# Modulation rows of a transformer-and-expert kernel computed as columns and carried to all partitions through DRAM

## The chip, the cores and the metric

The kernel runs on one core of a Trainium2 chip. The metric is the device time of one execution in microseconds (us); less is better. The kernel before takes 2819.86 us (median of 3 runs, 2818.37 to 2821.85).

## The reference

Two blocks follow each other on 256 tokens of width 1024 in float32. The first block has two layers of three sublayers (feed-forward, mixer, feed-forward) with keys and values shared from a stage between the layers. The second has a convolution, a differential attention and, after each of the two, a layer of experts chosen by keys (16384 experts, 16 per head, 8 heads). Each sublayer is modulated: from a conditioning vector c a shift, a scale and a gate of 1024 values each are computed by a product with a wide matrix.

```python
mods = jnp.split(c_act @ cond_w[layer] + cond_b[layer], 3 * N_SUBLAYERS, axis=-1)

def sublayer(x, shift, scale, gate, g_pre, g_post, fn, res_weight):
    h = rmsnorm(x, g_pre) * (1 + scale[:, None, :]) + shift[:, None, :]
    return x + res_weight * gate[:, None, :] * rmsnorm(fn(h), g_post)

def ada_mod(c, w, b):                                   # second block
    m = jax.nn.silu(c) @ w + b
    shift, scale, gate = jnp.split(m, 3, axis=-1)
    return shift[:, None, :], 1.0 + scale[:, None, :], 1.0 + gate[:, None, :]
    ...
    h = x * scale + shift
    x = layer_norm(DEEPNORM_ALPHA * x + gate * f, ln_g[i, 0], ln_b[i, 0])
```

The change concerns how these shifts, scales and gates are computed and brought to where they are used. Nothing else of the arithmetic changes.

## The kernel before, in words

**Stages.** The program is a list of stages numbered 0 to 7: feed-forward (0), gated linear attention (1), feed-forward (2), the shared keys and values (3), feed-forward (4), latent attention (5), feed-forward (6), convolution (7). A tail holds the experts (8), the attention (9) and the experts again (10). A feed-forward stage streams 11 tiles of 2 MB of gate-and-up weights and then 6 tiles of down weights through a ring of four slots in SBUF. SyncE issues these loads (`fill`, L561). TensorE computes 22 "units" of 16 matmuls each into three PSUM banks `psW` in turn (the loop with L955), and then the product with the down weights (`project`, L894). ScalarE applies the activation (L1599) and VectorE multiplies gate and up (L2194) and so frees the bank (`unit_stored`).

**Modulation work.** The product of c with the wide matrix is cut into 60 pieces of 512 outputs (1024 x 512 weights, 2 MB), and each piece into two halves of 1 MB. The table `beside` says beside which feed-forward stage (0, 2, 4 or 6) a piece is computed: 16, 14, 14 and 16 pieces. GpSimd issues the loads of the halves into three 1 MB buffers (`modulation_weights`, L496 and L500; two in `mring`, one in `M`), each after the half that was there three halves ago has been used (`m_used`). VectorE computes them between its multiplications, four halves in three units (`halves_done`, `half_step`). A piece is named (stage, j): j = 0, 1 is the shift, 2, 3 the scale, 4, 5 the gate.

There are two ways to compute a piece:

- **As a column** (32 pieces: shift and scale of stages 1 to 7 and 9). The weights come transposed, outputs on the partitions. `half_column` runs two operations of 128 x 1024 with an accumulated sum (L2048), which give two columns of 128 outputs each, and adds the bias columns (L2052). The result lies in `col`, eight values per partition for a vector of 1024, and is used where features lie on the partitions.
- **As a row** (28 pieces: all gates, and all of stages 8 and 10). VectorE accumulates eight products of 128 x 512 in `macc` (L2028, L2030) and adds the bias in one partition (L2035). What remains is a sum over the 128 partitions, which TensorE makes with a matmul against a matrix of ones, so that the sum lands in all partitions of the bank `psM`. For the 18 pieces used in stages 0 to 8 this is `sum_row` (L744), placed between units of the feed-forward stage or inside `project`, and VectorE moves the result to its place in `M` (`store_row`, L2097 and L2100, for a gate of stages 0 to 6 with the norm gain that GpSimd spread there before, `gate_gain`, L549). For the last 10 pieces ("late") the matmuls (L1396) stand in the first phase of the tail and ScalarE moves the result (`late_row`).

**Tail.** GpSimd issues 512 gathers of 1 MB (L662) into eight buffers, each after the one before in its buffer has been used; VectorE makes dot products (L2536), ScalarE weights them (L1722 to L1729), TensorE sums the gathered rows (L1303). Other work of TensorE (queries, attention) is interleaved.

The order on each engine is the order of the program text. The waits between engines are semaphores.

Of the kernel before, what the change touches and what calls it, by code (L numbers as in the profile page):

```python
# [29 lines left out]
F32 = mybir.dt.float32  # L30
# [55 lines left out]

class Turn:
# [33 lines left out]
def _program(nc, ctx, a, out, stages):  # L121
# [20 lines left out]
    small = sb("small", [P, 320])  # L142
# [80 lines left out]
    given_cols = arena[:, 14080:14296]  # L223
    cond_row = [M[:, 0, 0, :], p_diag[:].rearrange("p n t -> p (n t)")]
    col_bias = given_cols[:, 0:160].rearrange("p (n v k) -> p n v k", n=10, v=2)
    col_gain = given_cols[:, 160:216].rearrange("p (n k) -> p n k", n=7)
    col = small[:, 160:320].rearrange("p (n v k) -> p n v k", n=10, v=2)
# [29 lines left out]
    b_loaded = [sem(f"b_loaded{i}") for i in range(2)]  # L257
    g_loaded = [sem(f"g_loaded{i}") for i in range(2)]
    ln_loaded = sem("ln_loaded")
# [7 lines left out]
    m_stored = sem("m_stored")  # L267
# [36 lines left out]
    late_summed = sem("late_summed")  # L304
    late_stored = sem("late_stored")
# [139 lines left out]
    def mod_bias(st):  # L445
        n = st.n
        if n < 7:
            layer, s = (0, n) if n < 3 else (1, n - 4)
            return a["cond_b"][layer][3 * D * s:3 * D * (s + 1)]
        i, m = divmod(n - 7, 2)  # L450
        return a["ada_b_2"][i, m]


    def rows_of(n, lo, hi):
        return [(every[n], j) for j in range(lo, hi)]

    beside = {0: rows_of(0, 4, 6) + rows_of(1, 0, 6) + rows_of(2, 0, 4) + rows_of(3, 0, 4),
              2: rows_of(2, 4, 6) + rows_of(4, 0, 4) + rows_of(5, 4, 6) + rows_of(5, 0, 4) + rows_of(8, 2, 4),
              4: rows_of(4, 4, 6) + rows_of(6, 0, 4) + rows_of(7, 0, 4) + rows_of(9, 0, 4),
              6: rows_of(6, 4, 6) + rows_of(7, 4, 6) + rows_of(8, 4, 6) + rows_of(9, 4, 6) + rows_of(8, 0, 2)  # L460
              + rows_of(10, 0, 6)}
    pieces = [row for n in (0, 2, 4, 6) for row in beside[n]]
    as_row = [j >= 4 or st.n in (8, 10) for st, j in pieces]
    row_pieces = [piece for piece, row in zip(pieces, as_row) if row]
    col_pieces = [piece for piece, row in zip(pieces, as_row) if not row]
    late_pieces = [(st, j) for st, j in row_pieces if st.n > 8 or (st.n == 8 and j >= 4)]
    summed_pieces = [piece for piece in row_pieces if piece not in late_pieces]

    def rows_before(st):
        return sum(piece in summed_pieces for n, rows in beside.items() if n < st.n for piece in rows)  # L470

    def row_count(st, j):
        return summed_pieces.index((st, j)) + 1

    def col_count(st):

        return 4 + 2 * (col_pieces.index((st, 3)) + 1) if st.n else 4


    def halves_done(st, unit):  # L480

        return min(2 * len(beside[st.n]), max(unit - 1, 0) * 4 // 3)

    def row_at(st, unit):

        return sum(piece in summed_pieces and 2 * r + 2 <= halves_done(st, unit - 2) for r, piece in enumerate(beside[st.n]))
# [4 lines left out]
    def modulation_weights(eng, i):  # L491

        st, j = pieces[i // 2 - 1] if i >= 2 else (stages[0], 0)
        q = i % 2
        if i >= 2 and (st, j) in col_pieces:
            eng.dma_start(half_rows[i % HALVES].rearrange("p k n -> p (k n)"), a["mod_t"][2 * col_pieces.index((st, j)) + q])\  # L496
                .then_inc(m_loaded[i % HALVES], 16)
            return
        r = 4 + row_pieces.index((st, j)) if i >= 2 else 0
        eng.dma_start(half_rows[i % HALVES].rearrange("p k n -> p (k n)"), a["row_t"][r, :, 2048 * q:2048 * (q + 1)])\  # L500
            .then_inc(m_loaded[i % HALVES], 16)
# [11 lines left out]
    def bias_row(eng, n):  # L513
        st, j = pieces[n]
        r = sum(as_row[:n])
        b = mod_bias(st).rearrange("(o n) -> o n", o=1)
        if r >= 2:
            before = [i for i in range(n) if as_row[i]][r - 2]
            eng.wait_ge(m_used, 2 * before + 4)
        eng.dma_start(brow[0:1, r % 2, :], b[:, HALF * j:HALF * (j + 1)])\  # L520
            .then_inc(b_loaded[r % 2], 16)

    def row_target(st, j):

        kind = j // 2
        if st.n >= 9:
            m = (M_at, M_p1)[st.n - 9][:, kind]
        elif st.n == 8 and kind == 2:
            m = M_at[:, 0]
        else:  # L530
            m = M[:, st.n % 2, kind]
        return m[:, (j % 2) * HALF:(j % 2 + 1) * HALF]
# [7 lines left out]
    gate_before = {2: 0, 4: 2, 5: 1, 6: 4}  # L540
    gates_loaded = {0: 16, 2: 32, 4: 48, 6: 64, 1: 16, 5: 32}

    def gate_gain(eng, st):

        par = st.n % 2
        if st.n in gate_before:
            eng.wait_ge(x_ready, x_count(gate_before[st.n] + 1))
# [121 lines left out]
    def _(pool):  # L669
# [28 lines left out]
        for n, (st, j) in enumerate(pieces):  # L698
            if st.n < 7 and j == 4:
                gate_gain(pool, st)  # L700
# [3 lines left out]
            if as_row[n]:  # L704
                bias_row(pool, n)
# [2094 lines left out]
```

## Time and profile before

| | us |
|---|---|
| Runs: median (lowest, highest) | 2819.86 (2818.37, 2821.85) |
| Profiled execution, span from first to last instruction | 2816.4 |
| TensorE matmul busy | 2553.4 (91%) |
| VectorE busy | 1565.9 (56%) |
| ScalarE busy | 635.3 |
| GpSimd busy | 668.6 |
| DMA, mean over the span | 333 GB/s, 938.33 MB |

The span is the only time that the profile gives for its execution; the runs' median is 3.5 us above it. A busy share says how long an engine works, not whether the program waits for it; that is read from the chain that ended last. Stages 0 to 7 fill the time up to about 1376 us; the tail fills the rest.

### The profile page before, as it was taken

How to read it: one execution, taken by the hardware profiler on the slowest of the kernel's cores; microseconds unless marked ns; L12 is line 12 of the kernel's file. 1: busy time of each engine (PE TensorE's matmuls, PEld its weight loads, DVE VectorE, ACT ScalarE, POOL GpSimd, SP SyncE). 2: the span in 40 equal slices, each digit the busy share in tenths (PEclk: the TensorE clock that was granted, in tenths of full speed). 3: DMA queues.
4: the chain of work that ended last, by engine and by line, in shares of the span. 5: the costliest groups of instructions: out<-in, count | busy, mean ns of one | idle time of the engine just before them, and what ended most of it. 6: DMA issues, size and time to landing. Idle time of an engine off the chain costs nothing.

```text
span 2816.4 us, 26912 instructions
## 1 busy us (share of the span) xinstructions
PE 2553.4 (91%) x9987; PEld 1595.6 (57%) x9987; DVE 1565.9 (56%) x3441; ACT 635.3 (23%) x1837; POOL 668.6 (24%) x687
## 2 busy tenths in 40 slices
PE   8999999999999999999999887999869989777776
PEld 6874558856884678758665333645425636322222
DVE  4562135524451546713688875365785666974544
ACT  1001210001000220000133433253333533332222
POOL 1110000100010001100243444243443333544332
PEclk9999999999999999999999999999999999999999
DMA  9894426845783548946799999999999999999997
GB/s 394 346 363 146 190 93 262 354 183 202 298 350 132 194 157 338 358 174 260 299 392 421 421 422 421 406 418 421 421 422 402 421 421 414 422 401 421 421 422 326
DMA packets 120409, 938.33 MB, mean 333 GB/s; under 512 B 14765, under 2 KB 16197, under 8 KB 18902
## 3 DMA queue, kind: packets, MB, share of 16 engines
q0 software_dynamic: 93344, 669.09, 58.5%
q1 hardware_dynamic: 26934, 267.52, 24.1%
q8 instruction: 79, 1.29, 0.2%
q14 instruction: 52, 0.43, 0.0%
HBM read 935.50 MB, written 1.05 MB: 333 GB/s over the span
## 4 chain that ended last, share of the span: by engine, by line
PE 65%; DMA 21%; DVE 7%; ACT 3%; issue 2%; SPq 1%; POOL 1%; DVEq 0%
PE psW L955 20%; DMA ring<-in_peer_uv_dram,lamt 19%; PE psF L1303 14%; PE psF L894 11%; PE psW L1414 4%; DVE ring L2536 3%; PE psW L864 2%; PE psW L834 2%; PE psW L1322 2%; PE psW L823 2%; PE psF L930 1%; PE psW L875 1%; PE psW L1426 1%; DMA mring<-in_tail_w_dram 1%; PE psF L1173 1%
## 5 line engine op out<-in xcount | busy, mean ns | idle before, releaser
L1303 PE MATMUL psF<-ring,p_diag 128*128 128x512 f32 x2048 | 954.2, 611 | 210.1 <-ACT p_diag L1729 208.1
L2536 DVE SCALAR_TENSOR_TENSOR ring<-ring,h 128x1024 f32<-128x1024 f32 x512 | 621.3, 1224 | 426.7 <-DMA ring<-in_peer_uv_dram,lamt 423.2
L662 POOL DMA_INDIRECT ring<-in_peer_uv_dram,lamt x512 | 579.7, 1132 | 1018.6 <-PE psF L1303 800.9
L1303 PEld LDWEIGHTS psF<-ring,p_diag 128*128 128x128 f32 x2048 | 378.8, 193 | 730.1 <-issue 392.4
L955 PE MATMUL psW<-hT,ring 128*128 128x256 f32 x2560 | 555.9, 379 | 0.1
L955 PEld LDWEIGHTS psW<-hT,ring 128*128 128x128 f32 x2560 | 486.1, 190 | 73.0 <-issue 7.7
L894 PE MATMUL psF<-ring,arena 128*128 128x512 f32 x704 | 303.5, 593 | 4.1 <-DVE arena L2194 4.1
L894 PEld LDWEIGHTS psF<-ring,arena 128*128 128x128 f32 x704 | 133.4, 190 | 172.1 <-issue 166.5
L1722 ACT ACTIVATE small<-small 128x2 f32<-128x2 f32 x255 | 51.6, 202 | 649.9 <-DVE ring L2536 649.8
L1729 ACT ACTIVATE p_diag<-ident,small 128x128 f32<-128x128 f32 x510 | 176.9, 394 | 8.3
L1599 ACT ACTIVATE arena<-psW 128x256 f32<-128x256 f32 x88 | 33.8, 384 | 595.8 <-PE psW L955 535.9
L2194 DVE TENSOR_TENSOR arena<-arena,psW 128x256 f32<-128x256 f32 x80 | 33.7, 421 | 234.4 <-ACT arena L1599 234.0
L1414 PEld LDWEIGHTS psW<-hT,mring 128*128 128x128 f32 x1024 | 120.3, 194 | 19.6 <-issue 11.5
L1414 PE MATMUL psW<-hT,mring 128*128 128x128 f32 x1024 | 121.3, 277 | 5.3 <-DMA mring<-in_tail_w_dram 5.2
L1725 ACT ACTIVATE small<-small,gout 128x1 f32<-128x1 f32 x510 | 122.4, 287 | 8.3
L500 POOL DMA_DIRECT2D mring<-in_row_t_dram x39 | 22.3, 572 | 342.8 <-DVE macc L2030 301.2
L2148 DVE RECIPROCAL small<-small 128x1 f32<-128x1 f32 x12 | 1.9, 155 | 182.0 <-ACT small L1584 182.0
L2048 DVE SCALAR_TENSOR_TENSOR mring<-mring,M 128x1024 f32<-128x1024 f32 x66 | 78.1, 1220 | 2.6 <-DMA mring<-in_mod_t_dram 2.6
L2000 DVE COPY arena<-psW 128x512 f32<-128x512 f32 (+5 forms) x48 | 29.9, 628 | 88.3 <-PE psW L864 52.3
L834 PE MATMUL psW<-hT,ring 128*128 128x128 f32 x640 | 73.8, 276 | 5.2 <-DVE hT L2112 5.2
L1583 ACT ACTIVATE h<-psF 128x1024 f32<-128x1024 f32 x12 | 12.3, 1025 | 293.5 <-PE psF L894 256.7
L834 PEld LDWEIGHTS psW<-hT,ring 128*128 128x128 f32 x640 | 72.2, 192 | 7.0 <-issue 4.0
(329 smaller groups left out, 2249.0 us busy)
## 6 DMA issues: line engine op xcount, KB each, us to landing
ring<-in_gu_t_dram SPq DMA_DIRECT2D x44, 2048.0 KB, 9.0
mring<-in_tail_w_dram SPq DMA_DIRECT2D x50, 1024.0 KB, 9.1
mring<-in_mod_t_dram POOLq DMA_DIRECT2D x43, 1024.0 KB, 7.0
ring<-in_down_t_dram SPq DMA_DIRECT2D x20, 2048.0 KB, 8.6
mring<-in_row_t_dram POOLq DMA_DIRECT2D x39, 1024.0 KB, 7.5
ring<-in_conv_in_t_dram SPq DMA_DIRECT2D x12, 2048.0 KB, 7.5
M<-in_mod_t_dram POOLq DMA_DIRECT2D x21, 1024.0 KB, 6.8
M<-in_row_t_dram POOLq DMA_DIRECT2D x19, 1024.0 KB, 7.5
```

The lines of the kernel that those rows point to most:

```text
L662: pool.indirect_dma_start(out=pair(n % PAIRS), out_offset=None, in_=rows, in_offset=bass.IndirectOffsetOnAxis(ap=s_idx[:, c:c + 1], axis=0 ...
L823: ins = pe.matmul(ps[:, t * P:(t + 1) * P], w[:, k, t * P:(t + 1) * P], hT[:, k, b * P:(b + 1) * P], start=(k == 0), stop=(k == KD - 1))
L834: ins = pe.matmul(ps[:, t * P:(t + 1) * P], w[:, k, t * P:(t + 1) * P], hT[:, k, b * P:(b + 1) * P], start=(k == t == 0), stop=(k == KD - ...
L864: ins = pe.matmul(ps[:, 0:n], lhs[:, k, b * P:(b + 1) * P], w[:, k, 0:n], start=(k == 0), stop=(k == kd - 1))
L894: ins = pe.matmul(psF[:, b, f * HALF:(f + 1) * HALF], lhs[:, k, b * P:(b + 1) * P], w[:, k % 4, f * HALF:(f + 1) * HALF], start=(k == 0), ...
L955: ins = pe.matmul(ps[:, part * T:(part + 1) * T], w[:, k, part * 256 + c * P:part * 256 + (c + 1) * P], hT[:, k, :], start=(k == 0), stop= ...
L1303: ins = pe.matmul(psF[:, b, f * HALF:(f + 1) * HALF], p_diag[:, n % PAIRS, :], row_v(n % PAIRS)[:, f * HALF:(f + 1) * HALF], start=(i == 0 ...
L1414: ins = pe.matmul(ps[:, t * P:(t + 1) * P], w[:, k, t * P:(t + 1) * P], hT[:, k, b * P:(b + 1) * P], start=(k == 0), stop=(k == KD - 1))
L1725: act.activation(p_w[:, c + s:c + s + 1], p_gel[:, c + s:c + s + 1], ACT.Copy, scale=s_g[:, b, i + s:i + s + 1]).then_inc(w_ready, 1)
L1729: act.activation(p_diag[:, c + s, :], ident[:], ACT.Copy, scale=p_w[:, c + s:c + s + 1])\
L2048: ins = dve.scalar_tensor_tensor(w[:, t, :], w[:, t, :], 1.0, cond_row[st.n >= 7], ALU.mult, ALU.mult, accum_out=dst[:, t:t + 1])
L2536: dve.scalar_tensor_tensor(row_u(c), row_u(c), 1.0, h[:, b, :], ALU.mult, ALU.mult, accum_out=p_dots[:, c:c + 1]).then_inc(dot_done, 1)
```

## The change

The 28 row pieces become column pieces: all 60 are computed by `half_column`. The bias columns and the norm gains of the gates (`col_post`) come with the other given columns, now 376 values per partition and not 216, and in `brow`. A vector that is needed in all partitions (14 of them, the table `ROWS`) is then written by GpSimd from `col` to a row of 4 KB in DRAM (`write_row`; eight values per partition that lie 512 bytes apart in DRAM, so 1024 separate elements) and read back to 128 partitions (`spread_row`, 512 KB). The matmuls with ones, `store_row`, `late_row`, the 28 bias loads and the 6 loads of `gate_gain` go away.

```diff
-    gate_before = {2: 0, 4: 2, 5: 1, 6: 4}
+    gate_before = {2: 0, 4: 2, 5: 1, 6: 4, 7: 5}
+ROWS = ((0, 2), (1, 2), (2, 2), (5, 2), (4, 2), (6, 2), (7, 2), (8, 2), (9, 2), (8, 0), (8, 1), (10, 0), (10, 1), (10, 2))
...
-    given_cols = arena[:, 14080:14296]
+    given_cols = brow[:].rearrange("p v n -> p (v n)")[:, 0:376]
...
+    def write_row(eng, r):
+
+        n, kind = ROWS[r]
+        eng.wait_ge(col_stored, 4 + 2 * (row_done(r) + 1))
+        eng.dma_start(a["rows"][r, :].rearrange("(k p) -> p k", p=P), col[:, n, kind, :],
+                      allow_slow_non_contiguous=True).then_inc(row_written, 16)
+
+    def spread_row(eng, r):
+
+        n, kind = ROWS[r]
+        eng.wait_ge(row_written, 16 * (r + 1))
+        if kind == 2 and n in gate_before:
+            eng.wait_ge(x_ready, x_count(gate_before[n] + 1))
+        eng.dma_start(row_target(n, kind), a["rows"][r:r + 1, :].to_broadcast([P, D])).then_inc(row_landed(n, kind), 16)
...
-        for n, (st, j) in enumerate(pieces):
-            if st.n < 7 and j == 4:
-                gate_gain(pool, st)
...
-            if as_row[n]:
-                bias_row(pool, n)
...
+        for n, piece in enumerate(PIECES + [None] * 4):
...
+            if piece:
+                for i in (2 * n + 2, 2 * n + 3):
+                    if i >= HALVES:
+                        pool.wait_ge(m_used, i - HALVES + 1)
+                    modulation_weights(pool, i)
+            if spread < written:
+                spread_row(pool, spread)
+                spread += 1
+            if written < len(ROWS) and row_done(written) <= n - 2:
+                write_row(pool, written)
+                written += 1
...
-        def sum_row():
-
-            n = rows_taken.n
-            row_bank()
-            pe.wait_ge(m_used, 2 * pieces.index(summed_pieces[n]) + 4)
-            pe.matmul(psM[:], ones[:], macc[:, n % 2, :], start=True, stop=True).then_inc(m_reduced, 1)
-            rows_taken.next()
...
-                    sums_at(st, 2 * s + c)
...
-                pe.matmul(psM[:], ones[:], row_target(st, j), start=True, stop=True).then_inc(late_summed, 1)
...
+            half_column(halves_taken.n + 2, every[PIECES[n][0]], PIECES[n][1], q)
...
+            if kind == 2 and st.n < 7:
+                link(ins)
+                ins = dve.scalar_tensor_tensor(dst, dst, 0.5 if st.kind == "ffn" else 1.0, col_post[:, st.n, k:k + 2],
+                                               ALU.mult, ALU.mult)
...
-            dve.wait_ge(m_stored, row_count(st, 5))
+            dve.wait_ge(g_loaded[par], gates_loaded[st.n])
```

**TensorE, in the feed-forward stage 0.** `psW0` to `psW2` are the banks of the units; `macc` holds a piece's products, `psM` their sum. Before:

```order
L955 MATMUL psW2<-hT,ring 128x256 x16
L955 MATMUL psW0<-hT,ring 128x256 x16
L744 MATMUL psM<-macc,ones 128x512
L955 MATMUL psW1<-hT,ring 128x256 x16
L744 MATMUL psM<-macc,ones 128x512
L955 MATMUL psW2<-hT,ring 128x256 x16
```

And in the changed kernel (L916 is the line that was L955):

```order
L916 MATMUL psW2<-hT,ring 128x256 x16
L916 MATMUL psW0<-hT,ring 128x256 x16
L916 MATMUL psW1<-hT,ring 128x256 x16
L916 MATMUL psW2<-hT,ring 128x256 x16
L916 MATMUL psW0<-hT,ring 128x256 x16
```

The two sums between units are gone, and nothing stands in their place. The same holds at all 18 places.

**GpSimd, in stage 6, where most vectors are carried.** In brackets stands the semaphore that the instruction waits for. Before, the loads of weights alternate with the 2 KB loads of biases:

```order
L520 DMA brow<-in_ada_b_2_dram 1x16x32 [waits m_used]
L500 DMA M<-in_row_t_dram 128x2048 [waits m_used]
L500 DMA mring<-in_row_t_dram 128x2048 [waits m_used]
L520 DMA brow<-in_ada_b_2_dram 1x16x32 [waits m_used]
L500 DMA mring<-in_row_t_dram 128x2048 [waits m_used]
L500 DMA M<-in_row_t_dram 128x2048 [waits m_used]
```

In the changed kernel the writes to DRAM (L523) and the reads to all partitions (L532) stand between them:

```order
L523 DMA modulation_rows<-small 128x8x1 [waits col_stored]
L477 DMA mring<-in_mod_t_dram 128x2048 [waits m_used] x2
L532 DMA M<-modulation_rows 128x1024 [waits row_written]
L523 DMA modulation_rows<-small 128x8x1 [waits col_stored]
L477 DMA M<-in_mod_t_dram 128x2048 [waits m_used]
L477 DMA mring<-in_mod_t_dram 128x2048 [waits m_used]
L532 DMA M<-modulation_rows 128x1024 [waits row_written]
L523 DMA modulation_rows<-small 128x8x1 [waits col_stored]
```

A read waits on GpSimd's queue until its write has landed, and the next loads of weights stand behind it.

## Rows read from the trace of the kernel before

**Rows 1.** The page: busy time, share of the span, instructions of each engine.
```profile
PE 2553.4 (91%) x9987; PEld 1595.6 (57%) x9987; DVE 1565.9 (56%) x3441; ACT 635.3 (23%) x1837; POOL 668.6 (24%) x687
```

**Rows 2.** The chain that ended last, stage 0: start us, us, what.
```profile
31.63 19.58 DMA ring<-in_gu_t_dram
...
51.25 27.89 PE psW L955 x128
79.14 0.86 PE psM L744 x2
80.00 6.91 PE psW L955 x32
86.91 0.86 PE psM L744 x2
```

**Rows 3.** The same chain in stage 6, at its last two sums.
```profile
1145.88 0.86 PE psM L744 x2
1146.74 6.91 PE psW L955 x32
1153.65 0.86 PE psM L744 x2
```

**Rows 4.** Costliest groups: the sums on TensorE, of stages 0 to 6 and late.
```profile
L744 PE MATMUL psM<-macc,ones 128*128 128x512 f32 x36 | 18.4, 592 | 0.0
...
L1396 PE MATMUL psM<-arena,ones 128*128 128x512 f32 x20 | 10.2, 592 | 0.0
```

**Rows 5.** Stretches of the tail: length, busy us of each engine, clock, DMA share, GB/s.
```profile
1600.00:1650.00 50.00, 40.76 (x91) 16.11 (x90) 45.79 (x147) 18.95 (x57) 25.12 (x21) 1.00 1.01 421
...
1700.00:1750.00 50.00, 35.92 (x78) 13.80 (x77) 30.36 (x48) 16.62 (x53) 21.24 (x20) 1.00 1.01 421
```

**Rows 6.** Groups by shape: column operations and row operations on VectorE.
```profile
L2048 DVE SCALAR_TENSOR_TENSOR mring<-mring,M 128x1024 f32<-128x1024 f32 x66 | 78.1, 1220 | 2.6 <-DMA mring<-in_mod_t_dram 2.6
...
L2030 DVE SCALAR_TENSOR_TENSOR macc<-mring,cact,macc 128x512 f32<-128x512 f32 x82 | 61.6, 751 | 2.8
...
L2052 DVE TENSOR_TENSOR small<-small,arena 128x2 f32<-128x2 f32 x64 | 10.3, 160 | 2.2
...
L2035 DVE TENSOR_TENSOR macc<-macc,brow 1x512 f32<-1x512 f32 x18 | 12.2, 680 | 0.6
...
L2028 DVE TENSOR_SCALAR macc<-mring,cact 128x512 f32<-128x512 f32 x14 | 6.7, 480 | 0.0
...
L2100 DVE SCALAR_TENSOR_TENSOR M<-psM,M 128x512 f32<-128x512 f32 x12 | 8.3, 691 | 0.1
```

**Rows 7.** VectorE in order of time, one unit of stage 4 with two column halves.
```profile
813.77 0.42 DVE L2194 TENSOR_TENSOR arena<-arena,psW 128x256 f32<-128x256 f32 x1 [4.00 <-ACT arena L1599]
814.11 1.22 DVE L2048 SCALAR_TENSOR_TENSOR M<-M,p_diag 128x1024 f32<-128x1024 f32 x1
...
819.01 0.16 DVE L2052 TENSOR_TENSOR small<-small,arena 128x2 f32<-128x2 f32 x1
820.67 0.42 DVE L2194 TENSOR_TENSOR arena<-arena,psW 128x256 f32<-128x256 f32 x1 [1.51 <-ACT arena L1599]
...
827.92 1.22 DVE L2048 SCALAR_TENSOR_TENSOR M<-M,p_diag 128x1024 f32<-128x1024 f32 x1
```

**Rows 8.** GpSimd in order of time: a load of weights and its wait.
```profile
816.77 0.53 POOL L496 DMA_DIRECT2D M<-in_mod_t_dram  x1 [6.38 <-DVE M L2048]
```

**Rows 9.** Issue to landing of L496's loads, L549's and L520's, one line each.
```profile
DMA to landing us min/median/max: 5.0/7.0/10.5
...
DMA to landing us min/median/max: 4.7/6.9/9.0
...
DMA to landing us min/median/max: 1.7/5.7/20.0
```

**Rows 10.** DMA from 1 to 4 us, small packets: queue: packets, MB, share.
```profile
q1 hardware_dynamic: 298, 0.02, 6.6%
```

**Rows 11.** The page: GpSimd's queue: packets, MB, share of 16 engines.
```profile
q0 software_dynamic: 93344, 669.09, 58.5%
```

**Rows 12.** GpSimd: a bias load of 16 pieces and the first gather.
```profile
31.64 0.52 POOL L520 DMA_DIRECT2D brow<-in_cond_b_dram  x1
...
1361.31 1.02 POOL L662 DMA_INDIRECT ring<-in_peer_uv_dram,lamt  x1 [170.41 <-DVE lamt L2516]
```

**Rows 13.** Stage 6 while the pieces run, as in rows 5.
```profile
1050.00:1200.00 150.00, 148.97 (x625) 118.23 (x624) 103.35 (x155) 6.91 (x18) 22.98 (x42) 1.00 0.90 350
```

**Rows 14.** TensorE in order of time, last work before the first row of rows 2 lands.
```profile
43.80 7.38 PE L834 MATMUL psW<-hT,ring 128*128 128x128 f32 x64 [0.54 <-DVE hT L2112]
```

More of the change, by code:

```diff
@@ L442, in output_done @@
             eng.wait_ge(w_used, outputs[st.w + LOADS[st.kind] - 1])
[L445 to L473, printed above, removed]
     def col_count(st):
-        return 4 + 2 * (col_pieces.index((st, 3)) + 1) if st.n else 4
+        return 4 + 2 * (PIECES.index((st.n, 3)) + 1) if st.n else 4
     def halves_done(st, unit):
-        return min(2 * len(beside[st.n]), max(unit - 1, 0) * 4 // 3)
-    def row_at(st, unit):
-        return sum(piece in summed_pieces and 2 * r + 2 <= halves_done(st, unit - 2) for r, piece in enumerate(beside[st.n]))
+        return min(2 * len(BESIDE[st.n]), max(unit - 1, 0) * 4 // 3)
     def have_weights(eng, i):
@@ L491, in modulation_weights @@
     def modulation_weights(eng, i):
[L493 to L501, printed above, removed]
+        if i >= 2:
+            w = a["mod_t"][i - 2]
+        else:
+            w = a["row_t"][0, :, 2048 * i:2048 * (i + 1)]
+        eng.dma_start(half_rows[i % HALVES].rearrange("p k n -> p (k n)"), w).then_inc(m_loaded[i % HALVES], 16)
     def first_row(n):
@@ L511, in first_weights, with row_done, row_target, row_landed @@
                 .then_inc(first_loaded[n + q if n == 3 else n], 16)
[L513 to L532, printed above, removed]
+    def row_done(r):
+        n, kind = ROWS[r]
+        return PIECES.index((n, 2 * kind + 1))
+    def row_target(n, kind):
+        if n >= 9:
+            return (M_at, M_p1)[n - 9][:, kind]
+        if n == 8:
+            return M_at[:, 0] if kind == 2 else M[:, 0, kind]
+        return M[:, n % 2, 2]
+    def row_landed(n, kind):
+        if n >= 9 or (n == 8 and kind == 2):
+            return late_rows_loaded
+        return next_rows_loaded if n == 8 else g_loaded[n % 2]
+    late_rows = sum(n >= 9 or (n == 8 and kind == 2) for n, kind in ROWS)
     def norm_rows(eng, n, landed):
@@ L757, in sum_columns @@
             ins.then_inc(m_reduced, 1)
-        def sums_at(st, unit):
-            for _ in range(row_at(st, unit) - row_at(st, unit - 1)):
-                sum_row()
         def first_modulation(n):
@@ L904, in project @@
                     ins.then_inc(w_used, 1)
-                if k % 4 == 3:
-                    late = rows_taken.n - rows_before(st)
-                    if k == 3:
-                        late = row_at(st, FT + 1) - late
-                    else:
-                        late = min(1, sum(piece in summed_pieces for piece in beside[st.n]) - late)
-                    for _ in range(late):
-                        sum_row()
             for b in range(TB):
```

161 lines of the change are left out of this document (41 added, 120 removed).

## The prediction

> **What bounds the kernel now.** I read the page first, then the chain that ended last, then the groups by shape, and at the end GpSimd's queue and the DMA in the stretches where the change puts work. TensorE is busy 91% of the span [rows 1], but that is a mean over two halves with different limits. In stages 0 to 7, up to about 1376 us, the chain is almost all TensorE: units of 6.91 us follow each other without a gap, and the sums over partitions are links of that chain, 0.86 us each [rows 2, 3]. In the tail the same look shows another bound: whether TensorE is busy 40.76 of 50 us, with late sums, or 35.92, without them, the DMA share is 1.01 and the rate 421 GB/s [rows 5]. There the gathers set the pace.
>
> **The sums that go, on TensorE.** The group of the sums has 36 records, two for each matmul, so 18 matmuls [rows 4]. All 18 stand in the chain, from 79.14 us in stage 0 to 1153.65 us in stage 6 [rows 2, 3]: 4 in stage 0, 6 in stage 2, 2 in stage 4, 6 in stage 6. Each puts the next unit 0.86 us later (80.00 less 79.14). When one goes, what is late next is again a unit of TensorE: VectorE sat idle for 4.00 us before the multiplication of a unit, and with two halves in the unit before still for 1.51 us [rows 7], so it follows a TensorE that is 0.86 us earlier. 18 x 0.86 = 15.5 us. I take all of it.
>
> **The late sums.** 20 records are 10 matmuls [rows 4], at 0.86 us each 8.6 us, and as many moves on ScalarE. They lie where DMA runs at 421 GB/s before, during and after them [rows 5]. The bytes of the tail do not change, so I take 0; the other end is 8.6 us of gain, if the stretch were bound by TensorE's order in spots.
>
> **VectorE.** A row piece costs one operation of 0.48, seven of 0.751 and a bias of 0.68, together 6.4 us; a column piece costs four of 1.220, four accumulator reads of 0.08 and two bias adds of 0.16, together 5.5 us [rows 6]. Over 28 pieces that is 179.6 less 154.8 us (the sum of the removed groups by their counts, 196 x 0.751 + 28 x 0.48 + 28 x 0.68, and 28 x 5.53). The 18 moves out of `psM` at 0.69 go too, 12.4 us [rows 6], and 24 small multiplications by the norm gain at 0.16 come, 3.8 us. Busy time falls by about 33 us, to about 1532. It is worth nothing by itself: VectorE waits for ScalarE and that for TensorE in each unit [rows 7].
>
> **GpSimd's queue and the DMA.** 28 bias issues of 0.5 us and 6 loads of 512 KB go; 14 writes and 14 reads of 512 KB come. The read is of the shape of the removed gain load: 0.53 us to issue, landed after 6.9 us [rows 9]. In stages 0, 2 and 4 there are as many reads as there were gain loads (2, 2, 1); in stage 6 there are 9 for 1. So stage 6 alone gets 8 x 0.524 = 4.2 MB more. It moves 350 GB/s at a share of 0.90 over 150 us [rows 13]; 28 GB/s more gives 0.97. That fits, with little room.
>
> The write is the operation that the trace does not show: 1024 elements of 4 bytes. From below: small packets cost 0.066 x 16 x 3 us / 298 = 10.6 ns each [rows 10], so 64 per engine take 0.7 us, and a 2 KB bias load landed after 5.7 us at the median, 1.7 at least [rows 9]. From above: the mean packet of GpSimd's queue costs 0.585 x 16 x 2816.4 / 93344 = 282 ns [rows 11]; at that price one write holds all engines for 18 us. I take the small packets, which are the nearer row in size: 1 us of the engines, landed in 3 to 6 us. The issue lies between the bias load's 0.52 us for 16 pieces [rows 12] and, if each element costs what one of those 16 does, 33 us; the load of 128 pieces takes 0.53 [rows 8], so the number of pieces hardly counts there, and I take 1 to 4 us.
>
> The Trainium skill speaks against this write: its page "DMA: Bandwidth & Descriptors" (section "Rules for kernel authors") says that a strided last dimension becomes one descriptor per element and should be rearranged, and under "Anatomy of one DMA" that most of about 2 us of fixed cost is the receipt from the written memory, with DRAM the slowest. The same page gives about 10.5 ns per packet, and the trace agrees with 10.6 (rows 10), though for reads. By that page a write would cost an estimated 2.7 us, which is inside what I took.
>
> What the queue must keep is the supply of halves. The buffer in `M` that was freed at 816.77 us [rows 8] was needed at 827.92 [rows 7], 11.2 us later, and a load takes 7.0 us [rows 9]: 4.2 us of room at this place, one of the tight ones. Behind it stands a second cover: if VectorE is late, TensorE waits only when a unit's bank is still full three units on, so after about 2 x 6.91 = 13.8 us less the 0.4 us of each of the two engines. In the program's order a read stands a whole piece, two halves or about 10 us, behind its write, so it does not wait if the write lands in 3 to 6 us. A write of 1 to 4 us to issue fits into the first cover, and anything up to some 17 us into both. I charge 0 and keep 5 us for stage 6 in the range.
>
> **The end of the pieces.** The last three or so vectors are written and read without weights between them; four DMAs of at most 7 us each one after the other end about 30 us later than GpSimd ends now. It waits 170.41 us for the first indices before its first gather [rows 12]. Nothing there is late.
>
> **The start.** The given columns grow by 160 values x 128 x 4 bytes = 82 KB ahead of the first weights, at 421 GB/s 0.2 us. The load that ends at 51.21 us heads the chain [rows 2], but TensorE is busy with the work before it until 43.80 + 7.38 = 51.18 [rows 14], so the 512 KB that no longer compete with it give nothing back. I charge 0.2 us.
>
> **Sum.** 2816.4 - 15.5 + 0.2 = 2801.1 us of span. The runs' median lies 3.5 us above the span, so 2804.6 us.
>
> **Rivals.**
> A. The late sums count too. For: TensorE stands at 40.76 of 50 us there. Against: 421 GB/s with them and without [rows 5]. It gives 2804.6 - 8.6 = 2796.
> B. Stage 6 eats part of the gain. Nine reads and nine writes come within about 140 us where the DMA share is 0.90 [rows 13]. If each write holds engines or queue for 6 to 10 us, GpSimd's loads come late, both covers are used up near the end of the loop, and TensorE waits 1 to 1.5 us per vector: 5 to 12 us lost, 2810 to 2817. Against: 10.6 ns per packet [rows 10].
> C. The writes become the bound, and the kernel is slower. The mechanism: GpSimd's queue in stage 6. With 18 us per write, 64 x 282 ns [rows 11], two pieces of weights (4.2 MB), one write and one read need 10 + 18 + 1.2 = 29 us of the engines, and the ring tile that belongs to them half as much again as 5 us; the loop offers 20.7 us. About five writes lie in the loop, each 14 us too long, 70 us, of which the 13 us of bank cover and the first stage of the ring cover some 20: 50 us lost there, 35 net, 2840. It decides from about 10 us per write on. Nothing in the trace is that slow for small packets; but none of its small packets goes to DRAM.
> D. TensorE's 15.5 us are given back in the tail, since a transfer hides them: if the tail's start hung on something other than the convolution's end. Against: the first gather waits for the choice of the first indices, behind work that TensorE's chain releases [rows 12]. It gives 2820.
>
> **How the numbers follow.** Forecast 0.72, A 0.08, B 0.11, C 0.05, D 0.04. What a measurement can tell from no change is 0.2%, 5.6 us. The forecast and A are faster, B mostly; D is the same; C is slower. Faster 0.88, same 0.07, slower 0.05. The range takes the forecast with its open costs (5 us of stage 6, part of the late sums) and about half of B: 2798 to 2812. C is outside.
>
> **What would show it.** Right: no matmul into `psM` from `macc` in the trace; units of stage 0 at an even 6.91 us; stages 0 to 7 end 15 us earlier and the tail is as long as now, at 421 GB/s; VectorE busy about 1532 us, TensorE about 2529. The write's issue of 1 to 4 us and its landing under 8 us would confirm the price. Wrong: TensorE waiting for VectorE in stage 6, or VectorE for the halves (now 2.6 us in all for the buffers in `mring` [rows 6]); a tail that is shorter would speak for A, one that is longer for D.

## The result, and the profile after

The changed kernel takes 2844.47 us (median of 4 runs, 2840.83 to 2849.07); the kernel before, beside it, 2819.91. The ratio is 1.0088 [1.0074, 1.0102]: 0.9% slower, where 2804.6 and faster was forecast. The profiled execution's span is 2844.1 us, 27.7 more than before. Throughout, runs in which the chip itself was in a slower state are left out: one of the kernel `before_wown` below (2891.22 us) and two of the kernel before beside it.

The page of the changed kernel, busy times and the DMA total:

```profile
PE 2542.4 (89%) x9931; PEld 1592.1 (56%) x9931; DVE 1520.7 (53%) x3476; ACT 628.9 (22%) x1827; POOL 665.5 (23%) x681
...
DMA packets 121112, 942.59 MB, mean 331 GB/s; under 512 B 14445, under 2 KB 15877, under 8 KB 19606
```

VectorE is 45 us less busy than in [rows 1] and TensorE 11. The bytes went from 938.33 to 942.59 MB, the 4.2 MB that were reckoned. No engine has more to do, and the program takes longer. TensorE should have been 24 us less busy (18 sums and 10 late ones); why it is only 11 is told at the end of this section. The chain that ended last (start us, us, what) shows where, first in stage 0:

```profile
31.46 20.36 DMA ring<-in_gu_t_dram
...
51.87 119.38 PE psW L916 x544
...
174.24 17.00 DMA mring<-in_mod_t_dram
191.29 0.04 issue
191.33 2.39 DVE mring L1953 x4
```

The units run without a sum between them for 119.38 us; compare [rows 2], where sums stood between. That is the step as forecast. Then a half of the modulation's weights, 17.00 us on its way, stands in the chain; before, no such load did. In stage 6 most of the chain consists of them:

```profile
1078.64 15.87 DMA mring<-in_mod_t_dram
...
1097.28 21.38 DMA mring<-in_mod_t_dram
...
1121.42 18.27 DMA mring<-in_mod_t_dram
...
1142.46 12.71 DMA mring<-in_mod_t_dram
...
1157.93 24.06 DMA mring<-in_mod_t_dram
...
1184.76 14.05 DMA mring<-in_mod_t_dram
...
1201.87 77.99 PE psF L863 x176
```

Here the chain in [rows 3] was TensorE's. From the first unit to the start of `project`, stage 6 took 144.3 us before (1031.94 to 1176.25) and takes 168.2 now (1033.67 to 1201.87): 24 us longer. Stage 4, with a single write (at 743.05 us), went from 140.9 to 139.1: its two removed sums are there in full, 1.7 us. Stage 0 took 142.8 us and takes 145.5, though it has four sums less; stage 2 took 142.6 and takes 141.6, though six sums (5.2 us) are gone. The first gather is issued at 1389.11 us against 1361.31 [rows 12], 27.8 us later: the whole loss lies ahead of the tail, and the tail is as long as before.

The groups on the loads' and the writes' lines (count: ns min/median/max; what the engine waited for; issue to landing) say what became slow. The write, L523:

```profile
L523 POOL DMA_DIRECT2D modulation_rows<-small x14: 911/911/920, 85.5 to 1258.6; - x14
...
  POOL arena L532: 55.5, 5
  POOL M L532: 50.2, 9
...
DMA to landing us min/median/max: 12.4/16.1/23.5
```

The loads of weights, L477:

```profile
  DVE mring L1953: 150.7, 36
  DVE M L1953: 67.5, 18
...
DMA to landing us min/median/max: 5.0/10.1/24.1
```

A write is issued in 0.91 us and lands after 16.1 us at the median, where 3 to 6 were taken. GpSimd stands 105.7 us in all before its reads until the writes have landed. VectorE waits 218 us for halves; before, it was 2.6 for the column halves [rows 6] and 5.1 for the others. A half lands after 10.1 us at the median instead of 7.0 [rows 9]. And the stretches of four microseconds behind the first write, issued at 85.50 us (length, busy of each engine, clock, DMA share, GB/s), show that not only the queue is held:

```profile
88.00:92.00 4.00, 4.00 (x20) 3.54 (x19) 2.87 (x6) 0.38 (x1) 0.12 (x1) 1.00 0.96 408
92.00:96.00 4.00, 4.00 (x21) 3.51 (x20) 0.21 (x1) 0.38 (x1) 0.43 (x1) 1.00 1.34 101
96.00:100.00 4.00, 4.00 (x20) 3.54 (x19) 2.66 (x6) 0.00 (x0) 0.53 (x1) 1.00 0.63 31
100.00:104.00 4.00, 4.00 (x21) 3.51 (x20) 2.82 (x6) 0.38 (x1) 0.71 (x2) 1.00 0.42 100
```

The rate falls from 408 to 31 GB/s, and it is low for some 8 to 10 us. This is the rate of all queues together, SyncE's weights included. Not every write falls into such a deep hole: behind the others that were read in the same way, the lowest stretch of four microseconds lies between 23 and 127 GB/s. Packets of the other transfers are held meanwhile: of the 8 KB packets, 242 took over 2 us in this trace, up to 10.3, and 2 did before (the median is 0.31 us in both). In stage 6, with six writes issued in the stretch, the same stretch as [rows 13] reads:

```profile
1050.00:1200.00 150.00, 126.76 (x565) 109.67 (x563) 64.06 (x134) 6.89 (x18) 20.28 (x34) 0.93 0.95 297
```

DMA share 0.95, not lower than before, at 297 GB/s, not 350; and TensorE, which was idle for 1 us, now is for 23 us. What it waits for stands in its two groups of the feed-forward stages, units and down product (the last numbers: idle us before them, and who ended it):

```profile
L916 PE MATMUL psW<-hT,ring 128*128 128x256 f32 x2560 | 559.9, 382 | 13.9 <-DVE arena L2086 11.6
...
L863 PE MATMUL psF<-ring,arena 128*128 128x512 f32 x704 | 309.8, 603 | 23.2 <-DVE arena L2086 23.2
```

So TensorE hardly ever waits for its own tiles of the ring (2.1 us); it waits for VectorE, which waits for halves. The same groups show a second loss: a matmul takes 382 and 603 ns at the mean, where it was 379 and 593. While TensorE stands idle the granted clock falls to its lower level, 1.2 GHz (0.50), and the first matmuls after the gap still run at it. This is the longest gap, 13.4 us before stage 6's `project`:

```profile
1193.00:1197.00 4.00, 0.00 (x0) 0.00 (x0) 0.00 (x0) 0.00 (x0) 1.78 (x3) 0.50 0.39 98
...
1201.00:1205.00 4.00, 3.13 (x4) 1.50 (x5) 0.78 (x4) 0.00 (x0) 0.53 (x1) 0.50 0.97 409
```

### The profile page after: what moved, and what is told of

Its sections match the earlier page's. It is cut to its first block, busy times and chain, and to the rows that moved or that the text cites. A ratio compares the mean times of both kernels' runs of the same rounds, so it can differ in the third digit from the quotient of the medians.

```text
span 2844.1 us, 26771 instructions
## 1 busy us (share of the span) xinstructions
PE 2542.4 (89%) x9931; PEld 1592.1 (56%) x9931; DVE 1520.7 (53%) x3476; ACT 628.9 (22%) x1827; POOL 665.5 (23%) x681
## 2 busy tenths in 40 slices
DMA packets 121112, 942.59 MB, mean 331 GB/s; under 512 B 14445, under 2 KB 15877, under 8 KB 19606
## 4 chain that ended last, share of the span: by engine, by line
PE 57%; DMA 28%; DVE 8%; ACT 3%; issue 2%; SPq 1%; POOL 1%; DVEq 0%; POOLq 0%
DMA ring<-in_peer_uv_dram,lamt 19%; PE psF L1263 14%; PE psW L916 11%; PE psF L863 11%; DMA mring<-in_mod_t_dram 5%; PE psW L1366 4%; DVE ring L2421 3%; PE psW L833 2%; PE psW L803 2%; PE psW L792 2%; PE psW L1282 2%; DMA M<-in_mod_t_dram 1%; DVE mring L1953 1%; PE psF L891 1%; PE psW L844 1%
## 5 line engine op out<-in xcount | busy, mean ns | idle before, releaser
L916 PE MATMUL psW<-hT,ring 128*128 128x256 f32 x2560 | 559.9, 382 | 13.9 <-DVE arena L2086 11.6
L916 PEld LDWEIGHTS psW<-hT,ring 128*128 128x128 f32 x2560 | 490.1, 192 | 82.7 <-issue 6.5
L863 PE MATMUL psF<-ring,arena 128*128 128x512 f32 x704 | 309.8, 603 | 23.2 <-DVE arena L2086 23.2
L477 POOL DMA_DIRECT2D mring<-in_mod_t_dram x80 | 42.4, 530 | 734.5 <-DVE mring L1953 732.8
L1953 DVE SCALAR_TENSOR_TENSOR mring<-mring,M 128x1024 f32<-128x1024 f32 x96 | 113.7, 1221 | 71.0 <-DMA mring<-in_mod_t_dram 70.9
L1953 DVE SCALAR_TENSOR_TENSOR mring<-mring,p_diag 128x1024 f32<-128x1024 f32 x64 | 75.8, 1221 | 79.8 <-DMA mring<-in_mod_t_dram 79.8
L477 POOL DMA_DIRECT2D M<-in_mod_t_dram x40 | 21.2, 530 | 341.1 <-DVE M L1953 316.7
L1535 ACT ACTIVATE h<-psF 128x1024 f32<-128x1024 f32 x12 | 12.3, 1024 | 310.2 <-PE psF L863 273.5
```

The costliest lines, as they stand in the source:

```text
L863: ins = pe.matmul(psF[:, b, f * HALF:(f + 1) * HALF], lhs[:, k, b * P:(b + 1) * P], w[:, k % 4, f * HALF:(f + 1) * HALF], start=(k == 0), ...
L916: ins = pe.matmul(ps[:, part * T:(part + 1) * T], w[:, k, part * 256 + c * P:part * 256 + (c + 1) * P], hT[:, k, :], start=(k == 0), stop= ...
L1953: ins = dve.scalar_tensor_tensor(w[:, t, :], w[:, t, :], 1.0, cond_row[st.n >= 7], ALU.mult, ALU.mult, accum_out=dst[:, t:t + 1])
```

## The experiments

Fourteen kernels ran. Three theories stood at the start: the **hold** (theory 1, or competition), in which each write takes the DMA engines from all other transfers; the **queue** (theory 2), in which GpSimd stands at a read until its write has landed, with the weights behind it; and the **rest** of the change (theory 3: the eight more reads). Times are to be compared by their ratios to the kernel before, since each group of runs has its own runs of that kernel beside it.

**The same values in pieces of 32 bytes.** The layout of the weights, biases and gains of the 14 vectors is given in another order, so that partition p holds the outputs 8p to 8p+7. The write is then 128 pieces of 32 bytes.

```diff
-        eng.dma_start(a["rows"][r, :].rearrange("(k p) -> p k", p=P), col[:, n, kind, :],
-                      allow_slow_non_contiguous=True).then_inc(row_written, 16)
+        eng.dma_start(a["rows"][r, :].rearrange("(p k) -> p k", p=P), col[:, n, kind, :]).then_inc(row_written, 16)
```

> The changed kernel with the weights of the 14 carried vectors laid out so that partition p holds the outputs 8p to 8p+7: each write is then 128 pieces of 32 bytes and not 1024 of 4; the result is the same. Theory 1 (the write's elements hold the DMA engines: in the changed kernel the rate fell to 25 to 55 GB/s for 8 to 10 us per write): 8 pieces per engine and not 64, some 1.2 us per write, 2803 to 2808 us. Theory 2 (GpSimd's queue stands still until the write has landed, 105.7 us in all, and the loads of weights behind it are issued late; the landing is a fixed price of writing to DRAM): 2835 to 2845. Theory 3 (the reads to all partitions and their 4.2 MB more are what costs): 2840 to 2848.

Measured 2802.28 us (2800.86 to 2805.74), ratio 0.9941 [0.9925, 0.9958]: 0.6% faster than before. Its write (L523), its page and its stage 6:

```profile
L523 POOL DMA_DIRECT2D modulation_rows<-small x14: 550/550/550, 84.2 to 1190.0; - x14
...
DMA to landing us min/median/max: 5.2/8.5/11.0
```

```profile
PE 2531.5 (90%) x9931; PEld 1586.3 (57%) x9931; DVE 1519.9 (54%) x3476; ACT 629.0 (22%) x1827; POOL 660.2 (24%) x681
```

```profile
1050.00:1200.00 150.00, 149.00 (x603) 114.30 (x603) 76.09 (x157) 6.53 (x17) 23.10 (x44) 1.00 0.92 365
```

The same bytes, the same reads, the same queue order, and TensorE is idle for only 1 us of the 150, at 365 GB/s. TensorE's busy time is 10.9 us less than in the changed kernel for the same matmuls; that much of the loss is the lower clock. Of the 43.0 us between the two spans (2844.1 and 2801.1), the other 32.1 are idle time of TensorE. The rest of the change costs nothing that shows, and this is the version to keep: it beats both kernels.

**No write at all.** The write and the wait for it are left out, and the reads fetch a row of the norm gains.

```diff
-        eng.dma_start(a["rows"][r, :].rearrange("(k p) -> p k", p=P), col[:, n, kind, :],
-                      allow_slow_non_contiguous=True).then_inc(row_written, 16)
```

> The changed kernel without the 14 writes and without the wait for them; the 14 reads of 512 KB stay but read a row of norm gains, so the modulation of gates and of stages 8 and 10 is left out. Theories 1 and 2: 2803 to 2807 us. Theory 3 (the reads): 2840 to 2848.

Measured 2801.78 us, ratio 0.9938 [0.9922, 0.9955]. It can't be told from the version with pieces of 32 bytes: 14 such writes cost nothing that can be measured.

**The writes alone, in the kernel before.** Thirteen writes from a constant of the kernel, at the places of the changed kernel; nobody waits for them.

```diff
+            if written < len(ROWS_DONE) and ROWS_DONE[written] <= n - 2:
+                pool.dma_start(a["rows"][written, :].rearrange("(k p) -> p k", p=P), cact[:, 0, :],
+                               allow_slow_non_contiguous=True).then_inc(row_written, 16)
+                written += 1
```

> The kernel before, with 13 writes of 1024 separate 4-byte elements to DRAM added at the places of the changed kernel's writes; nothing waits for them and nothing is read back. Theory 1: about 35 to 40 us slower than before, 2852 to 2860. Theory 2 and theory 3: 2819 to 2824, since there is neither a wait nor a read.

Measured 2835.31 us, ratio 1.0055 [1.0039, 1.0072]. The sign is that of the hold; the size is half of what was expected or less, which the last pair of experiments takes up. In this trace TensorE waits at one kind of instruction above all, the sums over partitions, which the changed kernel no longer has:

```profile
L753 PE MATMUL psM<-macc,ones 128*128 128x512 f32 x36 | 19.5, 625 | 13.4 <-DVE M L2104 10.6 <-DVE macc L2044 2.8
```

In the kernel before this group had no idle time [rows 4].

**Half the elements.** As before, but with `[:, 0:4]` of both sides, 512 elements.

> As the kernel before with 13 added writes, but of 512 elements each, 32 per engine. Theory 1: the engines are held half as long, 4 to 5 us, which is close to the 4 us of room that the buffers have, so the loss is less than half: 2824 to 2836. Theories 2 and 3: 2819 to 2824.

Measured 2832.92 us, ratio 1.0047 [1.0030, 1.0064]. The issue fell from 0.92 to 0.78 us and the median landing from 14.5 to 13.7. The time lies in the range that theory 1 gave, but so near to that of 1024 elements that the two can't be told apart, and the rate falls as deep (35 GB/s in its lowest stretch). So there is no sign of a price per element in this range; since a cost shows only once the room of the buffers is used up, the run can't exclude one.

**The changed kernel without the wait.** Its reads fetch the norm gains and don't wait for the writes, which stay.

```diff
-        eng.wait_ge(row_written, 16 * (r + 1))
```

> The changed kernel with its 14 scattered writes, but the 14 reads do not wait for them: they read a row of norm gains, so the modulation of gates and of stages 8 and 10 is left out. The writes alone cost 17 us where nothing waited for them (before_w1024), and the changed kernel stands 42 us above the one with 32-byte writes. If the other 25 us come from GpSimd's queue standing still behind each write: 2815 to 2825 us. If they come from the writes and reads competing for the DMA engines: 2838 to 2846.

Measured 2838.41 us, ratio 1.0060 [1.0044, 1.0077]. By the ratios that is 8 us less than the changed kernel, though the two intervals touch. If the queue alone were the cause, most of the loss would have come back; the hold is the larger part.

**The reads two pieces behind their writes.**

```diff
-            if spread < written:
+            if spread < written and n >= at[spread] + 2:
```

> The changed kernel with each read to all partitions issued two pieces (about 20 us) behind its write and not one; the result is the same. By the queue theory its wait is mostly gone: 2818 to 2828 us. By the competition theory nothing changes: 2838 to 2846.

Measured 2836.71 us, ratio 1.0054 [1.0037, 1.0071]. GpSimd's wait at the reads fell from 105.7 to 31.6 us, and the time by 9 to 10 us by the ratios, about as in the run before. So the queue's standing is worth some 8 us and the hold the rest.

**What makes the hold: DRAM, distance or number.** Four kernels with 13 writes of 1024 separate elements (12 into SBUF), placed as in the kernel of the writes alone. First 512 bytes between the elements, then the same elements into a scratch buffer in SBUF, where they lie 8 bytes apart in each partition:

```diff
-                pool.dma_start(a["rows"][written, :].rearrange("(k p) -> p k", p=P), cact[:, 0, :],
+                pool.dma_start(a["rows"][written, :].rearrange("(k p e) -> p k e", p=P, e=P)[:, :, 0], cact[:, 0, :],
```

> The kernel before with 13 added writes of 1024 elements of 4 bytes that lie 512 bytes apart in DRAM, so that no two share a block of 512. If what holds the engines are neighbours in one block of DRAM that are written at the same time from several engines: 2820 to 2824 us. If each element has its price: 2833 to 2838, as before_w1024 (2835).

```diff
-                pool.dma_start(a["rows"][written, :].rearrange("(k p) -> p k", p=P), cact[:, 0, :],
+                pool.dma_start(scrap[:, written, :].rearrange("p (k e) -> p k e", e=2)[:, :, 0], cact[:, 0, :],
```

> The kernel before with 12 added copies of 1024 separate 4-byte elements from SBUF to SBUF. If the hold is a matter of the number of elements: 2831 to 2837 us. If it is a matter of DRAM as the target: 2817 to 2822.

Measured 2819.31 us, ratio 0.9998 [0.9988, 1.0007], and 2819.36 us, ratio 0.9995 [0.9986, 1.0005]. Neither costs anything that can be measured. The number of separate elements is not the price. (Elements side by side in SBUF were not tried, so this pair alone doesn't tell the target from the distance.) Then 64 and 16 bytes between the elements (`e=16` and `e=4` in the same line):

> As the run with one element every 16 bytes, but one every 64 bytes of DRAM. Theory S (sharing some tens of bytes): 2817 to 2822, no dip. Theory B (sharing some hundreds of bytes): 2825 to 2838, dips remain. Theory A (only neighbours that touch): 2817 to 2822, no dip.

> The kernel before with 13 scattered writes of 1024 four-byte elements from GpSimd, one element every 16 bytes of DRAM (neighbours from different partitions); nothing waits for them or reads them. The same 1024 elements lying side by side cost 16.7 us in the median and stalled the DMA engines for some 8 us each; 512 bytes apart they cost nothing. Theory S (elements that share a small piece of DRAM, some tens of bytes, hold each other up): four share 64 bytes here instead of sixteen, so between 2822 and 2836, dips that remain. Theory B (it is a block of some hundreds of bytes that they share): as side by side, 2832 to 2838. Theory A (only exact neighbours, which touch, hold each other up): 2817 to 2822 and no dip.

Measured 2818.96 us, ratio 1.0000 [0.9990, 1.0010], and 2818.12 us, ratio 0.9995 [0.9985, 1.0005]. Four elements in 64 bytes cost nothing that can be measured as long as they lie 16 bytes apart. Of the theories named, only the one of exact neighbours stands. One rival to it is open: with 16 bytes between them the elements are also fewer per 64 bytes (4 and not 16), and a price that sets in only above some density would look the same. Neither pairs that touch nor elements 8 bytes apart were tried. A small rest may be left at 16 bytes: 25 of the 8 KB packets took over 2 us, against 136 side by side, 4 at 64 bytes, 6 at 512 and 2 in the kernel before. The two write groups on the DMA page (out<-in, count, KB each, median us to landing), side by side in DRAM:

```profile
modulation_rows<-cact POOLq DMA_DIRECT2D x13, 4.0 KB, 14.5
```

and 16 bytes apart:

```profile
modulation_rows<-cact POOLq DMA_DIRECT2D x13, 4.0 KB, 8.9
```

The same stretches behind the first write, side by side:

```profile
92.00:96.00 4.00, 4.00 (x21) 3.51 (x20) 0.66 (x2) 0.38 (x1) 0.00 (x0) 1.00 1.03 49
96.00:100.00 4.00, 4.00 (x20) 3.54 (x19) 3.96 (x8) 0.00 (x0) 0.53 (x1) 1.00 0.46 45
```

and 16 bytes apart:

```profile
92.00:96.00 4.00, 4.00 (x21) 3.51 (x20) 0.44 (x2) 0.38 (x1) 0.00 (x0) 1.00 0.90 205
96.00:100.00 4.00, 4.00 (x20) 3.54 (x19) 3.97 (x8) 0.00 (x0) 0.53 (x1) 1.00 1.02 401
```

**Whose neighbours, and whose queue.** Side by side again, but eight neighbours from one partition:

```diff
-                pool.dma_start(a["rows"][written, :].rearrange("(k p) -> p k", p=P), cact[:, 0, :],
+                pool.dma_start(a["rows"][written, :].rearrange("(p k) -> p k", p=P),
+                               ones[:, 0:16].rearrange("p (k e) -> p k e", e=2)[:, :, 0],
```

> The kernel before with 13 writes of 1024 four-byte elements that lie side by side in DRAM, as in the costly one, but in which eight neighbours come from one partition (read from a constant at every second element, so that they stay separate elements). If what costs is that neighbours in DRAM are written from different partitions: 2817 to 2823. If what costs is any separate four-byte elements side by side: 2830 to 2838, with dips of the DMA rate to some 50 GB/s behind each write, as with one element from each partition in turn.

Measured 2841.85 us (2839.92 to 2846.39), ratio 1.0084 [1.0064, 1.0104]: it costs, if anything more. That the neighbours come from different partitions is not the cause. And the costly write issued by SyncE, among its weights:

```diff
+                if j in WRITES.get(st.n, ()):
+                    sp.dma_start(a["rows"][written.n, :].rearrange("(k p) -> p k", p=P), cact[:, 0, :],
+                                 allow_slow_non_contiguous=True).then_inc(row_written, 16)
```

> The kernel before with 13 writes of 1024 four-byte elements side by side in DRAM, neighbours from different partitions, as in the costly one, but issued on SyncE's queue, behind the weight transfers, instead of GpSimd's. If it is the target and the shape of the write that stall the DMA engines: 2828 to 2845 (one more thing that stands in the weights' queue), with dips as before. If it is how GpSimd's queue hands such a write over: 2817 to 2823 and no dip.

Measured 2846.99 us, ratio 1.0096 [1.0079, 1.0113], just above the range for it, with a median landing of 28.6 us and a rate down to 41 GB/s. GpSimd's queue is not the cause; what the write does at its target is.

**Why it costs more in the changed kernel.** The writes alone cost about 16 us in the kernel before, but the changed kernel is 42 us behind its form with pieces of 32 bytes. The 18 sums are put back into both as matmuls whose result nothing uses:

```diff
+                    if 2 * s + c in SUMS[st.n]:
+                        pe.matmul(psM[:], ones[:], macc[:, 0, :], start=True, stop=True)
```

> The changed kernel with 18 matmuls of 128x512 put back between units of the feed-forward stages (4 in stage 0, 6 in stage 2, 2 in stage 4, 6 in stage 6), with a result that nothing uses. The same writes cost 16.7 us in the kernel before and 42 us in the changed one against its repaired form. Theory T (where the writes starve the weights, TensorE waits for DMA, and work taken off it there is worth nothing): the 18 matmuls of 0.86 us each cost next to nothing here, only the 1.7 us of stage 4, so 2844 to 2850 beside 2844.5 for the changed kernel. Rival R (the time of TensorE is on the path in both kernels, and the larger cost comes from the reads and the queue): 15.5 us more, 2858 to 2862.

> The repaired kernel (writes in pieces of 32 bytes) with the same 18 matmuls put back. Both theories: here TensorE sets the pace of the stages, so all of 18 x 0.86 us comes back, 2816 to 2820 beside 2802.3. If it is less, then part of the gain of the repaired kernel does not come from the removed sums.

In the changed kernel: 2837.95 us, ratio 1.0062 [1.0046, 1.0079]. In the one with pieces of 32 bytes: 2817.54 us, ratio 0.9987 [0.9977, 0.9997]. By the ratios the 18 matmuls cost 13 us in the latter (0.9987 less 0.9941, of 2820; 15.5 was reckoned and lies within the error) and nothing in the former. There it is even 7 us faster with them (1.0062 against 1.0088; the intervals overlap from 1.0074 to 1.0079, so this is likely and not certain). Rival R had 15.5 us more there and falls; theory T had the direction, but its range began at 2844. Stage 6 of the changed kernel with the sums put back:

```profile
1050.00:1200.00 150.00, 137.50 (x583) 113.32 (x582) 67.34 (x140) 6.92 (x18) 20.29 (x34) 0.94 0.97 315
```

TensorE works 11 us more in these 150 us than in the changed kernel, which has less to do. The two profiled spans (2831.4 and 2844.1) differ by 12.7 us, and some 7 of these are the clock: TensorE is busy for 2551.0 us, less 15.5 for the sums 2535.5, against 2542.4 for the same matmuls in the changed kernel. The waits of the down product for VectorE are shorter too, 11.0 us and not 23.2. Why the gaps are shorter with more work stays open; the weights arrive at other moments, and none of the runs holds that apart.

So the 42 us can be put together as an estimate: 16 us for the writes in a kernel whose TensorE is otherwise the bound; 13 us, because TensorE's saving can't be had where TensorE waits for VectorE, and that for weights; some 8 us for the queue that stands at the reads. That makes 37, and the 5 that are left are about as large as the error of such a sum. The parts are differences between kernels, and that they add up is not shown: the 16 us hold 13.4 of waiting at sums that the changed kernel doesn't have. The lower clock is no fourth part; its 11 us are spread over these. A cross-check: with the 18 matmuls in both, the two kernels with pieces of 4 and of 32 bytes are 21 us apart (1.0062 less 0.9987), and the writes alone and the queue make 24.

## Why the prediction was wrong, step by step

**The failed step: the write's price.** "1 us of the engines, landed in 3 to 6 us" was worked out from small packets that are read from DRAM [rows 10] and from small loads into SBUF [rows 9]. Measured: 16.1 us to land at the median, and the transfers of all queues nearly stopped for 8 to 10 us behind many of the writes. None of the rows was of a write to DRAM; the text itself said so under rival C ("none of its small packets goes to DRAM") and then charged the price of reads all the same. The upper bound, 18 us of engines, came from a row with nothing in common with the write, and it was too high by a factor of two, while the lower one, 0.7, was too low by more than ten. "The nearer row in size" was the wrong nearness: how the elements lie at the target counted, not their size or number. For elements that lie apart, and for those in SBUF, charging nothing was right, though even these landed after 8.6 to 8.9 us and not 3 to 6. So "I charge 0" failed with the price that it was worked out from, and the forecast's own sign of being wrong, VectorE waiting for the halves, came: 218 us.

**Rival C** happened: 2840 forecast, 2844.5 measured, with a chance of 0.05. Its mechanism was right in the main (writes that hold the engines, GpSimd's queue late, stage 6 the worst), but that its number is so near is partly luck, since its terms are not those measured. It had 18 us of the engines per write, and the rate was low for 8 to 10. It had the price per packet, and half the elements cost nearly as much as all. It had about five costly writes; six were issued before stage 6's `project`, and three more behind. And it had the loss in stage 6 alone, 50 us there; that stage lost 24, and stages 0 and 2, with two writes each, lost what their removed sums had saved. Its threshold of about 10 us per write was not tested.

**The cover.** "Anything up to some 17 us into both" spoke of one write that delays GpSimd's queue. But a half is now also slow on its way: with 4.2 us of room [rows 7, 8] halves came 3 us later at the median and took up to 24, and in stage 6 a write follows the one before after 14 to 33 us. The cover itself was described rightly: TensorE's waits are for banks that VectorE had not freed (23.2 and 11.6 us), hardly for the ring. A cover that was worked out for one late issue does not hold for a transfer that slows all loads again and again.

**The clock, a term that was not in the sum.** TensorE's busy time was forecast at 2529 us and is 2542.4: the gaps brought the clock down, and 10.9 us of the loss are matmuls at the lower level. Without gaps there is no such term, as the version with pieces of 32 bytes shows.

**TensorE, 15.5 us for 18 sums: right**, shown, where nothing stalls the loads, by the sums put back (13 us by the ratios, 18.5 by the spans 2819.6 and 2801.1) and by the version with pieces of 32 bytes: 2802.3 us where 2804.6 was forecast for a write that costs nothing. TensorE's busy time there is 2531.5, forecast 2529.

**VectorE, about 1532 us busy: 1520.7**, and worth nothing. The column pieces were reckoned right: added up over the groups, busy time falls by 37 us, and 33 was reckoned. The page's total, which is less than the sum of the groups (1565.9 against 1665.5) because instructions overlap, fell by 45.

**The late sums at 0: right** as far as the traces go. With the ten sums gone the tail is as long as before, and its rate is that of [rows 5]:

```profile
1600.00:1650.00 50.00, 38.23 (x81) 14.89 (x80) 45.84 (x129) 16.56 (x53) 26.86 (x20) 0.97 1.01 422
...
1700.00:1750.00 50.00, 37.31 (x82) 14.50 (x81) 24.96 (x41) 13.77 (x50) 20.84 (x21) 1.00 1.01 422
```

**The reads, 8 x 0.524 MB more in stage 6 at little cost: right**, 365 GB/s at a share of 0.92 in the version with pieces of 32 bytes. **The issue of 1 to 4 us: 0.91,** just under it. **The end of the pieces: right in effect.** GpSimd still waits 115.59 us before the first gather, so nothing there was late.

**The Trainium skill** ("DMA: Bandwidth & Descriptors", section "Rules for kernel authors") had warned of the strided last dimension, and following it would have avoided the loss. Its price for small descriptors did not say so: the estimate of 2.7 us per write stands against 16.1 measured. By the rule alone the elements 16 bytes apart and those in SBUF, as many descriptors, should cost as much, and the runs show no cost.

## What to carry to other kernels

A transfer that the trace does not contain is priced from one of the same direction and the same target, and if there is none, the range reaches to the expensive bound: a cheap row of another kind is no evidence. A write of separate 4-byte elements side by side in DRAM is to be avoided, at 2 KB as at 4 KB; a layout in which each partition owns 32 contiguous bytes took its cost away here, and that layout can be prepared with the weights. A saving on one engine is only had if that engine stays the bound, so a new stall costs itself and the saving, and on TensorE the clock as well. The cost of a stall that was measured in one kernel need not be its cost in another.

## What the runs showed of the hardware

- 1024 elements of 4 bytes side by side in DRAM (4 KB) drop the rate of all queues together from about 410 GB/s to 30 to 50 behind the first write, for some 8 to 10 us, from GpSimd's queue as from SyncE's, and with neighbours from one partition as from several. 512 elements do nearly the same (35 GB/s).
- The same number of elements 16, 64 or 512 bytes apart in DRAM, or in SBUF, costs nothing that can be measured (in SBUF 8 bytes apart; side by side was not tried there). Where between 4 and 16 bytes the border lies in DRAM was not tried. What happens there in the memory no run shows; only the distance was tested.
- The write's own packets look cheap in the trace: 14 writes leave 224 records of 256 bytes, 79 ns at the median, and those of the writes 16 bytes apart have the same 79 ns. The hold shows only in the other transfers: 242 of their 8 KB packets take from 2 to 10.3 us, where the median is 311 ns; in the version with pieces of 32 bytes it is 2 packets. A stall of this kind is seen in the rate by stretches, not in the records of the write that causes it.
- In stage 6 TensorE's granted clock was 1.00 (2.4 GHz) in the stretches in which it worked without a gap; in the gap of 13.4 us it fell to 0.50 (1.2 GHz) and was still there when the work began again. In all, 9931 matmul records took 2542.4 us with such gaps and 2531.5 without.
